# Rotary embedding of queries and keys: who adds the cosine term, the matrix engine or the vector engine

## The reference

```python
def partial_rope(x, cos, sin):
    half = ROPE_DIM // 2
    x1, x2, xp = x[..., :half], x[..., half:ROPE_DIM], x[..., ROPE_DIM:]
    return jnp.concatenate([x1 * c - x2 * s, x1 * s + x2 * c, xp], axis=-1)
...
        qn = rmsnorm(heads(nq, NSA_HEADS), nsa_qnorm_g[i])
        q_rope = partial_rope(qn, cos, sin)
        k_sl = partial_rope(rmsnorm(heads(ksl, KVH), nsa_knorm_g[i, 1]), cos, sin)
        k_wn = partial_rope(rmsnorm(heads(kwn, KVH), nsa_knorm_g[i, 2]), cos, sin)
        o_slc = selected_attn(q_rope, k_sl, ...)
        o_win = window_attn(q_rope, k_wn, ...)
```

## Time and profile before

| | |
|---|---|
| median of 3 runs | 1197.81 us (1193.64 to 1198.2) |
| span of the profiled execution, first to last instruction | 1197.1 us |
| PE busy | 1108.9 us, 93% |
| DVE busy | 704.2 us, 59% |
| ACT busy | 579.7 us, 48% |
| share of PE in the chain that ended last | 74% |
| mean granted TensorE clock | 0.953 of full speed |

### The profile page before, as it was taken

One profiled execution on the slowest core, in us unless ns is written; L12 is line 12 of the kernel. 1 busy time (PEld: TensorE's weight loads), 2 busy tenths in 40 slices (PEclk: granted clock), 3 DMA queues, 4 the chain that ended last, 5 costly groups with the idle time before them and its releaser, 6 DMA issues.

```text
span 1197.1 us, 19879 instructions
## 1 busy us (share of the span) xinstructions
PE 1108.9 (93%) x8321; PEld 1037.9 (87%) x8321; DVE 704.2 (59%) x1009; ACT 579.7 (48%) x816; POOL 4.9 (0%) x13
## 2 busy tenths in 40 slices
PE   4999898798999889798989999999799999999997
PEld 4999676698999677798988999999786699999996
DVE  5556445647566445548685766666543646766674
ACT  4542435546432445545753644544542636455453
POOL 1000000000000000000000000000000000000000
PEclk8999899899998899899999999999996999999998
DMA  8541613135531612134554555556243323655530
GB/s 278 176 113 36 211 36 106 36 106 177 183 107 36 211 62 80 53 121 150 179 176 141 177 176 184 193 184 194 76 146 119 127 91 122 211 176 183 193 115 36
DMA packets 144740, 163.88 MB, mean 137 GB/s; under 512 B 6072, under 2 KB 135424, under 8 KB 144672
## 3 DMA queue, kind: packets, MB, share of 16 engines
q1 hardware_dynamic: 143752, 161.46, 42.0%
q10 hardware_dynamic: 632, 1.29, 0.3%
q0 software_dynamic: 288, 0.14, 0.0%
HBM read 161.84 MB, written 1.05 MB: 136 GB/s over the span
## 4 chain that ended last, share of the span: by engine, by line
PE 74%; DVE 11%; ACT 9%; DMA 2%; issue 2%; SPq 1%; ACTq 0%; DVEq 0%
PE ps L419 21%; PE ps L421 21%; PE ps L420 21%; DVE panels_low L1534 3%; ACT panels_high L1069 3%; PE ps L612 2%; PE ps L499 2%; ACT probs L1055 2%; PE ps L705 2%; PE ps L435 1%; DMA panels<-in_w_in 1%; DVE neg_max L1555 1%; DVE probs L1570 1%; PE ps L523 1%; PE ps L505 1%
## 5 line engine op out<-in xcount | busy, mean ns | idle before, releaser
L419 PE MATMUL ps<-input_high,panels_low 128*128 128x256 f32 x1792 | 523.6, 292 | 33.4 <-DVE input_low L1514 14.2
L420 PE MATMUL ps<-input_low,panels_high 128*128 128x256 f32 x1792 | 515.4, 288 | 0.0
L421 PE MATMUL ps<-input_high,panels_high 128*128 128x256 f32 x1792 | 515.4, 288 | 0.0
L1534 DVE TENSOR_TENSOR panels_low<-panels,panels_high 128x2048 fp32r<-128x2048 f32 (+1 forms) x146 | 330.3, 2265 | 287.5 <-ACT panels_high L1069 279.8
L419 PEld LDWEIGHTS ps<-input_high,panels_low 128*128 128x128 f32 x1792 | 352.1, 196 | 44.5 <-issue 31.2
L420 PEld LDWEIGHTS ps<-input_low,panels_high 128*128 128x128 f32 x1792 | 352.3, 197 | 0.8 <-issue 0.5
L421 PEld LDWEIGHTS ps<-input_high,panels_high 128*128 128x128 f32 x1792 | 351.9, 196 | 0.0
L1069 ACT CAST panels_high<-panels 128x2048 fp32r<-128x2048 f32 (+1 forms) x146 | 274.7, 1883 | 152.3 <-PE ps L421 133.2
L419 PE MATMUL ps<-ffn_hidden_high,panels_low 128*128 128x256 f32 x352 | 100.3, 285 | 4.0 <-DVE ffn_hidden_low L2014 4.0
L420 PE MATMUL ps<-ffn_hidden_low,panels_high 128*128 128x256 f32 x352 | 99.7, 283 | 0.0
L421 PE MATMUL ps<-ffn_hidden_high,panels_high 128*128 128x256 f32 x352 | 99.7, 283 | 0.0
(11 more groups left out here) (267 smaller groups left out, 1174.7 us busy)
## 6 DMA issues: line engine op xcount, KB each, us to landing
panels<-in_ffn_up SPq DMA_DIRECT2D x44, 1024.0 KB, 5.1
panels<-in_w_in SPq DMA_DIRECT2D x32, 1024.0 KB, 5.7
panels<-in_ffn_down SPq DMA_DIRECT2D x22, 1024.0 KB, 4.8
panels<-in_mix_w_in SPq DMA_DIRECT2D x20, 1024.0 KB, 5.3
panels<-in_w_out SPq DMA_DIRECT2D x8, 1024.0 KB, 5.3
panels<-in_w_pg SPq DMA_DIRECT2D x8, 1024.0 KB, 6.1
panels<-in_mix_w_out SPq DMA_DIRECT2D x8, 1024.0 KB, 5.8
panels<-in_w_pp SPq DMA_DIRECT2D x2, 1024.0 KB, 4.9
```

What stands on the lines that cost most here:

```text
L419: pe.matmul(dst, w[1], x[0], start=start, stop=False if not kw else True, **kw)
L420: pe.matmul(dst, w[0], x[1], start=False, stop=False if not kw else True, **kw)
L421: return pe.matmul(dst, w[0], x[0], start=False, stop=stop, **kw)
L1534: V.tensor_tensor(low_slots[slot][:, 0:size], raw[n % SLOTS][:, 0:size], high_slots[slot][:, 0:size].bitcast(F32), ALU.subtract).then_inc( ...
```

## The change

The identity matmuls are gone on PE. The banks now hold only the rotated sine terms. The steps "copy qr0" and "copy qr1" on ACT become steps "q_rotated" on DVE, which adds the cosine terms from `UW` to the bank and writes `q_rope`; "k_pad" moves from ACT to DVE, where its four copies become four additions of `UK` and the bank. Two waits are new on ACT: before it overwrites `UW` it waits for `qr1` to be taken out, and before it overwrites `UK` for `kr`.

```diff
                 for j in range(2):
                     begin(f"qr{j}_{l}", 1 + j)
-                    pe.matmul(ps[1 + j][:, :], ident, UW[:, j * 512:(j + 1) * 512], start=True, stop=False)
                     done(f"qr{j}_{l}", pe.matmul(ps[1 + j][:, :], const("rot"),
                                                  UW[:, 1024 + j * 512:1024 + (j + 1) * 512],
-                                                 start=False, stop=True))
-                    todo(("copy", f"qr{j}"))
+                                                 start=True, stop=True))
+                    todo(("q_rotated", j))
                 some(1)
                 pe.wait_ge(k_rope_ready, l + 1)
                 begin(f"kr_{l}", 4)
-                pe.matmul(ps[4][:, :], ident, UK[:, 0:512], start=True, stop=False)
-                done(f"kr_{l}", pe.matmul(ps[4][:, :], const("rot"), UK[:, 512:1024], start=False, stop=True))
+                done(f"kr_{l}", pe.matmul(ps[4][:, :], const("rot"), UK[:, 512:1024], start=True, stop=True))
                 todo(("k_pad",))
...
-                dest = {"nq0": QN[:, 0:512], "nq1": QN[:, 512:1024], "qr0": QR[:, 0:512], "qr1": QR[:, 512:1024],
+                dest = {"nq0": QN[:, 0:512], "nq1": QN[:, 512:1024],
...
-                    elif step == "k_pad":
-
-                        name = f"kr_{l}"
-                        full(act, name)
-                        src = v3(bank(name), 2)
-                        for g in range(2):
-                            s = src[64 * g:64 * g + 64]
-                            nc.scalar.copy(kz[0:64, :, 0, g, :], s)
-                            ins = nc.scalar.copy(kz[64:128, :, 1, g, :], s)
-                        ins.then_inc(free(name), 1)
...
                         drained(act, f"o1_{l}")
+                        drained(act, f"qr1_{l}")
                         f(SQ[:, 0:1024], QP[:, :], ACT.Square).then_inc(osq_ready, 1)
...
                         act.wait_ge(rope_ready, l + 1)
+                        drained(act, f"kr_{l}")
...
+                    elif kind == "q_rotated":
+                        name, s = f"qr{arg[0]}_{l}", slice(arg[0] * 512, (arg[0] + 1) * 512)
+                        full(dve, name)
+                        V.tensor_tensor(QR[:, s], UW[:, s], bank(name)[:, :], ALU.add).then_inc(free(name), 1)
+                    elif kind == "k_pad":
+
+                        name = f"kr_{l}"
+                        full(dve, name)
+                        for g in range(2):
+                            h = slice(64 * g, 64 * g + 64)
+                            for r in range(2):
+                                ins = V.tensor_tensor(kz[64 * r:64 * r + 64, :, r, g, :], v3(UK[:, 0:512], 2)[h],
+                                                      v3(bank(name), 2)[h], ALU.add)
+                        ins.then_inc(free(name), 1)
```

## The result

The changed kernel is slower. Its median is 1202.8 us over 6 runs (1199.6 to 1207.4), that of the kernel before beside it 1194.7 us over 6 runs (1193.4 to 1198.2); the ratio is 1.0061, 95% interval [1.0038, 1.0085]. The forecast was 1206.3 us and +8.5 us; by the two ratios the difference is +7.3 and +10.1 us.

A forecast was written before the change was run, and what follows sets the result against it. Two near-equal paths, ACT's copy of qr0 and DVE's level (6,1), were taken to bound the place of the change. Queue 3.8 plus clock 0.45 us, over two layers, gave +8.5 on 1197.8: 1206.3 us, range 1201.5 to 1211.

The forecast's parts named there:

- Which path binds: At the change, the chain runs over DMA, ACT's cast, DVE's split and level (6,1), with PE idle 1.30 us.
- Part 1: Identity matmuls on PE: removal saves 2.6 to 3.4 us per layer, all off the path, so 0 in the sum.
- Part 2: DVE's first addition waits behind two splits and level (6,1), so hgo0 starts at 135.85, +3.8 us per layer.
- Part 3: After hgo0's start: DVE's longer list stays covered by 1.4 us before the cross product, costing 0.
- nothing swallows it: Behind hgo0: no later wait absorbs the shift, as the next long DMA, at 261.54, starts where a PE product ends.
- The sign for the second layer: PE's first matmul of hgo0 in the second layer would stand at 402.5 plus the first layer's shift.
- Part 4: Half clock at hgo0's start after PE's idle time of nearly 8 us: +0.45 us per layer, between -1.5 and +2.4.
- The sum: Whole kernel: 2 x (3.8 + 0.45) = +8.5 us, giving 1206.3 us from a median of 1197.8.
- The clock did give back: Rival, recurrence's output and gate product: each layer sheds half-clock stretches, total 1202.5 or 1199.6 us, not slower; chance 0.15.
- The matmuls were not on the path: Rival claimed they were, before hgo0: bank 1 freed early, -5 to -7.8 us, about 1191.5; chance 0.05.
- The keys' additions did not outrun their cover: Rival claimed they would: DVE's level (7,1) ends too late for the cross product, +1.0 per layer, 1208.3; chance 0.05.

The follow-up runs named there:

- the keys' half: Kernel before, with only the keys' identity matmul removed and "k_pad" moved from ACT to DVE as four additions; 1193.8 us, ratio 1.0010.
- after_again: The changed kernel measured again with no edit, also called the yardstick; 1202.6 us over 6 runs, ratio 1.0085 to the kernel before.
- The filled kernel: Changed kernel plus eight unread matmuls of 512 columns in PE's idle time after the keys' rotation; 1199.9 us, ratio 1.0062 to the kernel before.
- the deferred kernel: Changed kernel with DVE's splits of panels hgo1 and hz0 moved behind level (7,1); 1184.5 us, ratio 0.9936 to the kernel before.
- half the deferral: Changed kernel with DVE's two splits moved only behind the queries' additions, ahead of level (7,0); 1192.8 us, ratio 0.9990 to the kernel before.
- with filling: Kernel before plus two unread matmuls in each of PE's two short waits for ACT; 1190.9 us, ratio 0.9977. The deferred kernel likewise: 1183.5 us, ratio 0.9920.

## Why the prediction was right

**Which path binds.** Right. The chain at the place runs over DMA, ACT's cast, DVE's split and level (6,1), as in the earlier trace rows, and in the changed kernel the addition is hung on its end.

**Part 1, the matmuls' worth.** Right: PE is through at 128.1 (forecast 127.3 to 128.2), and the run without them shows no gain.

**Part 2, the queue.** Right. Forecast 135.85 in the first layer, measured 135.78, with DVE 0.05 to 0.08 us earlier throughout. In the second layer hgo0 stands at 402.15, 3.77 us later than before when both are taken from DVE's first split (395.14 before, 394.86 after). The price of an addition, 0.69 us from the earlier trace rows, measured 0.68 (mean of the four); two overlapping records take 1.28.

**Part 3, the cover.** The list holds: DVE waits 1.31 us for PE before its last level, and ACT stands idle from 131.5 for 13.0 us. The keys' additions took 2.77 us for four, not 2.4; the upper bound, DVE's 687 ns for 128 partitions, was the right row, and half the partitions are no cheaper. DVE is through at 140.3 (forecast 140.1). That the cover is thin is shown by the keys' half alone. One sentence of this part is wrong by a little: "nothing swallows it". In the kernel before PE waits 0.40 us before 273.42 for a panel of the DMA at 261.54. With the change PE comes later and finds that panel ready, so 0.6 us of the first layer's shift is gone there, in both profiles of the changed kernel (3.5 us becomes 2.9, and 5.5 becomes 4.9); the second layer has no such loss.

**The sign for the second layer.** The prediction wanted hgo0 there at 402.5 plus the first layer's shift, some 406. The first profile has it at 402.15, and so misses the sign; the second (`after_again`) has it at 407.10. In the first the shift is still 3.5 us behind the layer, at 265. Then come the 0.6 us, and between 294 and 298 another 1.4 us go, where the kernel before has a stretch of 3.4 us at half clock that this execution lacks. So what was lost on the way is mostly the clock of that one execution, and the delay of each layer is to be read within the layer.

**Part 4, the clock.** The mechanism was right: 3.7 us at half clock at hgo0's start in the first profile, within the 3.3 to 5.4, and a stretch shed behind it. In the first layer the shift is 3.74 at hgo0, 5.15 at the cross product, and 3.52 at the gate product behind the output: +1.4 for the half-clock start, -1.6 for the output at full clock. The second layer has the same pattern (+1.4, -1.6). Between these two executions the clock term is thus about -0.2 per layer, where I took +0.45. The second profile of the changed kernel tells another story for its first layer: the shift is 3.76 at hgo0, 5.85 at the cross product and 5.85 at the gate product, so nothing is shed and the term is +2.1; in its second layer it is -0.25. The four layers average +0.3 and span most of the range of -1.5 to +2.4. That +0.45 comes close to this average is luck: it was the middle of a wide range, and no row chose it. Over the runs the mean clock fell from 0.959 to 0.953, which at 0.78 us for 0.001 would be 3 to 5 us in all. That overstates it, since a part of the new half-clock time falls into the idle time ahead of hgo0 and costs nothing (the window from 130.2 to 135.7 at 0.75 is 2.75 us of it per layer). The filled kernel and the yardstick put the clock's share at 2.7 us, with overlapping intervals; by the first measurement it would be nothing. The size of this term in the total stays open. One slip of working stands in that part: with one half in place of 0.44 the middle of -1.65 and +2.7 is +0.53, so the sum would be some 0.15 us higher, and not 0.4.

**The sum.** The size, +8.5, lies between the two measurements, +7.3 and +10.1. The time of 1206.3 was 3.5 us high for another reason, the term of the sum on which all rests: I took the median of three runs, 1197.8, for that of the kernel, and the six runs beside the changed kernel have 1194.7. I also took the profiled execution as 0.7 us under the median. The 67 further runs, in three groups, have medians of 1191.8 to 1192.9, and in later runs a span lies 1.9 us under the time of its own execution. The profile I worked from was thus of about 1199 us (an estimate, 1197.1 + 1.9). Its mean clock, 0.953, was on the page, and I had nothing to compare it with.

**The rivals.** The clock did give back in the profiled layers, but the total is slower by over 0.5% in both measurements. The matmuls were not on the path; the deferred kernel shows what it takes to put them there, and its 7.6 us under the kernel before lie within the -5 to -7.8 that the rival was priced at. The keys' additions did not outrun their cover, but they do once PE is early (the keys' half, half the deferral).

## What to carry to other kernels

When a step moves to another engine, ask first what stands ahead of it in that engine's list and who waits for what it frees: 0.69 us of work cost 3.8 us per layer here because it stood behind two panel splits and a level, and the same instructions in another order were 0.6% faster than the kernel before instead of 0.6 to 0.9% slower. Work taken from an engine that then waits is worth nothing until the wait is moved too, and both gates of the path have to be moved. Before comparing two profiles look at their mean clocks, and compare single stretches with a common starting point.

## What the runs showed of the hardware

The granted clock goes with most of the scatter of this kernel on one core: 10 us between the shortest and the longest of 67 runs, with a correlation of -0.95. I had not expected that PE's short waits of 1.7 and 1.8 us matter so much: without filling, half clock followed the first in 6 layers of 18 and the second in 17 of 22, with filling in none of 4, and the kernel gained 2.7 us [1.0, 4.4] by it. The Trainium skill ("TensorE: Matmul & The Clock Gate", Why this matters for your kernels) warns that longer idle gaps between bursts bring the half rate back. The changed kernel agrees, with its gap of 7.6 us; for the waits of 1.7 and 1.8 us, after which half clock followed often but not always, the measurement goes further than the rule, and it decides.

An addition of 64 partitions by 512 elements took as long as one of 128 partitions: 683 ns (mean of eight) against 682 (mean of four) in the changed kernel. The four for the keys start 0.7 us apart and take 2.77 us in all, while the two for the queries overlap by 0.1 and take 1.28.
